# A three-layer network in split float32: the third pair's first weight chunk ahead of the first pair's convolution on ScalarE and VectorE

## The reference, cut to what matters

```python
def conv_glu_ffn(x, norm_g, w_up, conv_w, conv_b, w_down):
    S = x.shape[1]
    h = rms_norm(x, norm_g) @ w_up
    hp = jnp.pad(h, ((0, 0), (CONV_W - 1, 0), (0, 0)))
    c = conv_b
    for j in range(CONV_W):
        c = c + conv_w[j] * hp[:, j:j + S]
    gate, up = jnp.split(c, 2, axis=-1)
    return x + (jax.nn.silu(gate) * up) @ w_down
```

## Time and profile before

| what | value |
|---|---|
| time, median of 3 executions | 1035.68 us (1035.67 to 1037.07) |
| span of the profiled execution | 1034.1 us |
| TensorE (PE) busy | 1007.7 us, 97% |
| VectorE (DVE) busy | 747.2 us, 72% |
| ScalarE (ACT) busy | 626.6 us, 61% |
| GpSimd (POOL) busy | 353.4 us, 34% |
| transfers | 183.45 MB, mean 177 GB/s |

### The profile page before, as it was taken

The page is one execution under the profiler, slowest core; times in us unless marked ns, Lnnn a source line. Parts: engine busy times, 40 slices in busy tenths (PEclk is TensorE's granted clock), DMA queues, the critical chain, the costliest instruction groups (busy, mean ns, idle before and its releaser), DMA issues.

```text
span 1034.1 us, 15900 instructions
## 1 busy us (share of the span) xinstructions
PE 1007.7 (97%) x6476; PEld 903.5 (87%) x6476; DVE 747.2 (72%) x1009; ACT 626.6 (61%) x880; POOL 353.4 (34%) x189
## 2 busy tenths in 40 slices
PE   7999999999998899999999999999999899999997
PEld 7889988888987798888888888888999698888886
DVE  5886999874577789988548766654799887656543
ACT  6776677663477477776436554544669866555531
POOL 1062176640000025665102545510148323555300
PEclk9999999999999999999999999999999999999999
DMA  9633575537441346656553655556342257565341
GB/s 345 223 127 124 220 265 205 199 132 256 147 163 42 121 146 209 238 177 209 190 200 123 244 204 171 195 203 219 122 154 98 83 171 255 184 202 183 144 164 41
DMA packets 27143, 183.45 MB, mean 177 GB/s; under 512 B 3008, under 2 KB 3136, under 8 KB 5824
## 3 DMA queue, kind: packets, MB, share of 16 engines
q1 hardware_dynamic: 26496, 181.40, 49.6%
q10 hardware_dynamic: 576, 1.05, 0.3%
HBM read 181.39 MB, written 1.05 MB: 176 GB/s over the span
## 4 chain that ended last, share of the span: by engine, by line
PE 82%; DVE 8%; ACT 5%; issue 2%; POOL 1%; DMA 1%; SPq 0%; DVEq 0%; POOLq 0%; ACTq 0%
PE psum L335 82%; DVE wlo L1563 2%; ACT whi L1030 1%; POOL Y L2244 1%; ACT Pb L1164 1%; DVE bias L1569 1%; DVE Pb L1694 1%; DMA gain_x<-in_x 1%; DVE Pb L1566 1%; DVE QK L1569 0%; DVE QR L1563 0%; DVE G L1563 0%; DVE Cb L1569 0%; ACT Ob L1372 0%; ACT PT L1030 0%
## 5 line engine op out<-in xcount | busy, mean ns | idle before, releaser
L335 PE MATMUL psum<-G,whi 128*128 128x512 f32 (+1 forms) x1856 | 550.6, 358 | 7.7 <-DVE wlo L1563 7.7
L1563 DVE TENSOR_TENSOR wlo<-raw,whi 128x2048 fp32r<-128x2048 f32 (+1 forms) x170 | 388.2, 2298 | 178.8 <-ACT whi L1030 178.8
L335 PE MATMUL psum<-G,wlo 128*128 128x256 f32 x1568 | 442.0, 282 | 0.0
L1030 ACT ACTIVATE whi<-raw 128x2048 fp32r<-128x2048 f32 (+1 forms) x170 | 315.9, 1871 | 149.5 <-PE psum L335 138.9
L335 PEld LDWEIGHTS psum<-G,whi 128*128 128x128 f32 x1856 | 329.6, 189 | 61.6 <-DVE G L1569 6.4
L335 PEld LDWEIGHTS psum<-G,wlo 128*128 128x128 f32 x1568 | 296.8, 189 | 0.1
L335 PE MATMUL psum<-A2room,whi 128*128 128x512 f32 (+1 forms) x784 | 228.5, 354 | 0.0
L2244 POOL TENSOR_TENSOR A2room<-Ab,A2room 128x512 fp32r<-128x512 f32 x44 | 141.3, 3211 | 130.9 <-ACT A2room L1030 130.9
L335 PE MATMUL psum<-A2room,wlo 128*128 128x256 f32 x656 | 184.6, 281 | 0.0
L335 PEld LDWEIGHTS psum<-A2room,whi 128*128 128x128 f32 x784 | 138.3, 188 | 20.9
L2244 POOL TENSOR_TENSOR Ab<-Cb 128x512 f32<-128x512 f32 x44 | 113.4, 2578 | 107.5 <-ACT Cb L1073 107.1
(11 more groups left out here) (192 smaller groups left out, 1035.9 us busy)
## 6 DMA issues: line engine op xcount, KB each, us to landing
raw<-in_wst SPq DMA_DIRECT2D x165, 1024.0 KB, 5.0
bias<-in_bias_c SPq DMA_DIRECT2D x1, 2048.0 KB, 9.4
raw<-in_wst SPq DMA_DIRECT2D x3, 512.0 KB, 8.1
raw<-in_wst ACTq DMA_DIRECT2D x4, 256.0 KB, 6.2
out<-bias SPq DMA_DIRECT2D x4, 256.0 KB, 2.1
gain_x<-in_x SPq DMA_DIRECT2D x3, 256.0 KB, 6.6
bias<-in_bias_a SPq DMA_DIRECT2D x1, 512.0 KB, 7.5
bias<-in_invcnt SPq DMA_DIRECT2D x1, 512.0 KB, 7.8
```

What stands on the lines that cost most here:

```text
L335: return pe.matmul(o, a, b, start=start, stop=stop, skip_group_check=True)
L1030: return act.activation(o, i, ACT.Copy)
L1563: return dve.tensor_tensor(o, a, b, op)
```

## The change

On ScalarE `high(c0 + 4)` moves from behind the four t2 of pair 0 to in front of them, right behind the two `normal_high`. On VectorE `low(c0 + 4)` moves from between `taps(0, 1)` and `taps(0, 0)` to in front of both, right behind the two `normal_low`. This is done in F0 and F1 only (`conv is not None`); the other two FFNs keep their order. Nothing is added or removed, and the programs of TensorE, GpSimd and SyncE are the same.

```diff
@@ scalar, ffn
                 for p in range(FP):
-                    for i in ((2, 3) if p == 0 else (4, 5) if p == 1 else (2 * p + 3,)):
+                    for i in ((2, 3) if p == 0 else (2 * p + 3,) if p > 1 or conv is not None else (4, 5)):
                         high(c0 + i)
...
                         if p == 0:
                             normal_high(0)
                             normal_high(1)
+                            high(c0 + 4)
@@ vector, ffn
                 for p in range(FP):
                     b = p % 2
-                    for i in ((2, 3) if p == 0 else (4, 5, 6) if p == 1 else (2 * p + 3, 2 * p + 4)):
+                    if p == 1 and conv is not None:
+                        taps(0, 0)
+                    for i in ((2, 3) if p == 0 else (2 * p + 3, 2 * p + 4) if p > 1 or conv is not None else (4, 5, 6)):
                         low(c0 + i)
-                        if conv is not None and i == 4:
-                            taps(0, 0)
...
                         if p == 0:
                             normal_low(0)
                             normal_low(1)
+                            low(c0 + 4)
                         taps(p, 1)
```

## The result

The change makes the kernel slightly faster. Over 20 executions of each, the median is 1034.55 us (1034.06 to 1035.20) against 1036.80 us (1035.39 to 1037.57) before. The ratio of the times is 0.9981, with a 95% interval from 0.9975 to 0.9987: 0.19% less, 2.0 us, with 1.3 to 2.6 us inside the interval. (The two medians as such lie 2.25 us apart.) The forecast was 1034.1 us and 0.16%.

The account below looks back on a forecast made before the run. TensorE was taken as the bound, busy 1007.7 of 1034.1 us; closing gaps of 0.81 and 0.80 us saves 1.6 us, taking the median from 1035.68 to 1034.1 us, range 1033.1 to 1036.0.

Parts of the forecast that it names:

- The two gaps of 0.56 us in brackets: TensorE idle before the first G matmul in F0 and F1, released by VectorE's low(c0 + 4); both were to close.
- the bound at the seam: At chunk c0 + 4, TensorE's own products rather than VectorE would set the start, with 0.87 us to spare.
- `low(c0 + 4)` was forecast 1.6 us earlier: On VectorE in F1, the split ahead of the taps would end at 387.28 instead of 388.88.
- `low(c0 + 5)` was to stay: On VectorE in F1, the next split would start at 390.4 as before (390.36).
- The copy, the t2 and the other copies on ScalarE: In F1, high(c0 + 4) ends at 384.5, four t2 at 386.4, the next two copies at 390.1 as before.
- 0.81 and 0.80 us: Saving on TensorE from closing the gap before the first G matmul, in F1 and F0 respectively.
- The choice of starts over idle time as ruler: Sizing TensorE's two gaps by recorded starts gives 1.6 us, by modelled idle time 1.1 us; 1.6 was taken.
- the Trainium skill's rule that went with it: On TensorE, a matmul's drain overlaps the next one's fill; an isolated matmul can't hide it, so gaps exceed idle time.
- Had the layer swallowed what F0 gave: Rival: attention layer between the FFNs loses F0's 0.8 us, giving 1034.9 us; partly or wholly lost, chance 0.14.
- the median of the runs lies 1.58 us above the span; I take that as unchanged: Whole-kernel step from the profile's span to measured time: 1035.68 less 1.6 gives 1034.1 us.
- the slow rival: Chunk c0 + 5 becomes late for TensorE, up to 1041.9 us; large delays 0.03, small ones 0.02.
- 1.05 us of room: Margin between low(c0 + 5) being ready and TensorE needing it in F1, shrinking from 1.9 us but staying positive.

Follow-up runs that it names:

- e8: Changed kernel with low(c0 + 5) and low(c0 + 6) behind the two Hb and first four taps of pair 1; 1044.33 us, ratio to before 1.0076.
- e6: Kernel before with low(c0 + 4) behind all eight taps in both FFNs; 1040.57 us, ratio to before 1.0039.
- e9: Kernel before, unchanged, run and profiled once more; 1036.85 us, ratio to before 0.9998.
- e10: Kernel before with four added products in the mixer's idle stretch, overwritten by the real one; 1035.71 us, ratio to before 0.9994.

## Why the prediction was right

**The bound and the place.** The two gaps of 0.56 us in brackets were named, and both are gone. TensorE, not VectorE, is the bound at the seam after, as reckoned. The first `G` products start at 117.93 and 388.24 us where about 117.4 and 387.6 were forecast; 0.54 us of both differences is the later first norm.

**The engines' steps, in F1 from the first `Hb`.** `low(c0 + 4)` was forecast 1.6 us earlier: it stood 386.58 - 381.53 = 5.05 us behind the `Hb` and stands 3.47 behind now. `low(c0 + 5)` was to stay: 8.83 and 8.84 us. The copy, the t2 and the other copies on ScalarE came in the order and the lengths given. No wait appears for `c0 + 5`.

**The size.** 0.81 and 0.80 us were forecast, 0.82 and 0.86 measured alone, 1.51 to 1.65 together for a sum of 1.6. The choice of starts over idle time as ruler was the one that mattered, and the Trainium skill's rule that went with it (TensorE: Matmul & The Clock Gate, section Step-by-step: what each phase is for) agrees with what was saved. That the drain is what fills the 0.25 us between the two rulers was not measured.

**Carried through.** F0's share came through the attention layer: from F0's first `G` product to F1's are 271.00 us before (389.13 - 118.13) and 270.31 after (388.24 - 117.93), 0.69 less. Had the layer swallowed what F0 gave, the interval would have grown. It holds F1's gap, 0.73 by starts, and the 0.08 by which F0's first product has become shorter, 0.81 in all; over the three profiles of each order it is 271.09 and 270.26 us, 0.83 less. So nothing was lost in between, within the 0.1 us by which profiles of one kernel differ.

**What was not foreseen** is in what surrounds the sum. The step "the median of the runs lies 1.58 us above the span; I take that as unchanged" rested on three executions, two of them of the lower group, and on a span of an execution that need not be one of them: where time and span are of the same execution they lie 1.8 us apart (1034.77 and 1033.0). It gave 1034.1 for 1034.55. Two terms are missing from it, and they work against each other. Of the 1.84 us between the means, 0.74 are the upper group of before, which the changed kernel does not show. The 1.10 us that are left are some 0.5 less than the stretch gives, and in the chain of the profile after the first norm, ahead of both FFNs, is 0.54 us later than in the one before. So it is partly luck that 0.16% was forecast and 0.19% measured; that the sum of 1.6 us was right rests on the stretches and not on this agreement. Of the slow rival the condition was right (1.05 us of room reckoned, 1.1 found) and the price was not: it left out what TensorE's clock adds behind a long wait.

## What to carry to other kernels

Where an engine's hand-written list puts work with slack in front of what the bounding engine waits for, a swap is free, but both engines that make the operand have to be turned around: either half alone gained nothing. The gain is capped by the gap on the bounding engine (here 0.8 us for a chunk that is ready 1.6 us sooner), and the gap is measured from start to start. Before a median of three is taken as the base for a change of 0.2%, look for a second group of executions, and in their profiles at the granted clock behind each long wait of TensorE.

## What the runs showed of the hardware

- **A wait of 2.3 us costs the clock in part of the executions.** Same kernel, same place: with 2.31 us of idle time the granted clock fell to 0.50 (1.2 GHz), with 2.41 us it stayed 1.00. It cost 1.0 us of 1036. In e8, with waits of 3.1 us, the fall came in both FFNs and cost 1.65 us each; in e6's one profile, with waits of 2.14 and 2.15 us, it came in neither. What decides it in an execution was not shown.
- **The start is not the same in each profile.** TensorE's first products start 0.64 us apart by threes, and later ones 0.35 us. The change of pace comes at about 10.0 us in the profile before and at 12 us in the one after. The slices from 10 to 12 us (instructions of PE in parentheses), before:

```profile
10.00:11.00 1.00, 1.00 (x11) 1.00 (x10) 0.98 (x4) 1.00 (x3) 0.00 (x0) 1.00 1.01 414
11.00:12.00 1.00, 1.00 (x11) 1.00 (x10) 0.96 (x2) 1.00 (x3) 0.00 (x0) 1.00 1.13 451
```

and after:

```profile
10.00:11.00 1.00, 1.00 (x6) 1.00 (x6) 1.00 (x4) 1.00 (x3) 0.00 (x0) 1.00 1.00 406
11.00:12.00 1.00, 1.00 (x7) 1.00 (x6) 0.91 (x2) 1.00 (x3) 0.00 (x0) 1.00 1.13 459
```

The column of the granted clock says 1.00 in all four, though half the pace is what its lower level gives elsewhere. The Trainium skill (TensorE: Matmul & The Clock Gate, section What's actually happening) has it that the default state is throttled and activity releases the throttle; the pace agrees with that and the column does not. The first norm stands at 20.92 and 21.46 us, and in the other profiles between 20.58 and 21.56. It is late where the pace changes late: with the change at 11 us, in e9, it still stands at 20.80, and with the change at about 12 us at 21.3 to 21.6.

Whether the changed kernel starts later or only these executions did is not shown. Four of the five profiles of kernels with both halves of the move have the first norm at 21.28 to 21.56 us, and the fifth, e8, has it at 20.58; the four with the old order (before, e6, e9, e10) have it at 20.80 to 20.92. Nothing that was moved is carried out before the first norm. A real difference of about 0.5 us would account for the step from the 1.6 us of the stretch to the 1.10 us between the lower group's mean and the changed kernel's.
